# Sums of squares of the RMS norms: full-array matmuls against partial sums in the four column quarters of TensorE

## The reference, cut to what matters

```python
def _rmsnorm(x, w):
    xf = x.astype(jnp.float32)
    y = xf * lax.rsqrt(jnp.mean(xf * xf, axis=-1, keepdims=True) + RMS_EPS)
    return (y * w.astype(jnp.float32)).astype(x.dtype)

h = h + _mixer(_rmsnorm(h, norm_mix_w[l]), ...)          # norm 0
h = h + _swiglu(_rmsnorm(h, norm_ffn_w[l]), ...)         # norm 1
h = _rmsnorm(h, norm_final_w)                            # folded into norm 2
h = _rmsnorm_2(x, mix_norm_g[layer]); x = x + mixer(h)   # norms 2 and 4
h = _rmsnorm_2(x, mlp_norm_g[layer]); x = x + mlp(h)     # norms 3 and 5
```

## Time and profile before

| | |
|---|---|
| median of 3 runs | 1178.59 us (1178.41 to 1178.78) |
| profiled execution, its own time | 1178.25 us |
| its span in the profile | 1176.5 us |
| mean granted TensorE clock | 0.977 of full speed |
| PE busy | 1122.0 us (95%) |
| DVE busy | 745.9 us (63%) |
| ACT busy | 508.6 us (43%) |

### The profile page before, as it was taken

The page is one execution under the profiler, slowest core; times in us unless marked ns, Lnnn a source line. Parts: engine busy times, 40 slices in busy tenths (PEclk is TensorE's granted clock), DMA queues, the critical chain, the costliest instruction groups (busy, mean ns, idle before and its releaser), DMA issues.

```text
span 1176.5 us, 21013 instructions
## 1 busy us (share of the span) xinstructions
PE 1122.0 (95%) x8656; PEld 1068.6 (91%) x8656; DVE 745.9 (63%) x813; ACT 508.6 (43%) x506; POOL 6.0 (1%) x6
## 2 busy tenths in 40 slices
PE   8999998899999999998998999999988999999998
PEld 7998885788989999988887999999978999999998
DVE  5764747576756666668746565555479776655563
ACT  5523332433544444455484444333443455434331
POOL 0000001000000000000000000000000000000000
PEclk8999999899999999999999999999898999999999
DMA  9673243134427565664423464654253435564630
GB/s 299 188 211 108 90 143 108 44 130 154 129 72 210 166 203 170 191 201 150 150 95 108 143 215 158 199 177 145 85 165 112 139 108 176 183 211 157 203 107 36
DMA packets 162590, 177.63 MB, mean 151 GB/s; under 512 B 4800, under 2 KB 148288, under 8 KB 162536
## 3 DMA queue, kind: packets, MB, share of 16 engines
q1 hardware_dynamic: 160704, 174.56, 46.9%
q10 hardware_dynamic: 1832, 2.30, 1.0%
HBM read 175.27 MB, written 1.57 MB: 150 GB/s over the span
## 4 chain that ended last, share of the span: by engine, by line
PE 79%; DVE 12%; ACT 5%; issue 2%; DMA 2%; ACTq 0%; SPq 0%; DVEq 0%
PE proj L417 48%; PE aux L778 20%; DVE wlo L1409 4%; DVE f L1412 2%; DVE f L1409 2%; PE aux L474 2%; ACT whi L1035 1%; PE aux L705 1%; DMA gamma_rows<-f 1%; DVE f L1415 1%; PE aux L688 1%; PE aux L585 1%; PE aux L574 1%; DMA f<-in_x_dram 1%; PE aux L698 1%
## 5 line engine op out<-in xcount | busy, mean ns | idle before, releaser
L417 PE MATMUL proj<-u,whi 128*128 128x256 f32 (+1 forms) x2912 | 538.7, 286 | 11.2 <-DVE wlo L1409 4.1
L1409 DVE TENSOR_TENSOR wlo<-raw,whi 128x2048 fp32r<-128x2048 f32 (+2 forms) x176 | 374.2, 2126 | 159.7 <-ACT whi L1035 151.7
L417 PEld LDWEIGHTS proj<-u,whi 128*128 128x128 f32 x2912 | 455.9, 191 | 20.3 <-issue 8.0
L417 PE MATMUL proj<-u,wlo 128*128 128x256 f32 (+1 forms) x1456 | 413.7, 284 | 0.0
L1035 ACT ACTIVATE whi<-raw 128x2048 fp32r<-128x2048 f32 (+3 forms) x174 | 311.6, 1791 | 124.8 <-PE proj L417 56.0
L417 PEld LDWEIGHTS proj<-u,wlo 128*128 128x128 f32 x1456 | 279.0, 192 | 0.0
L778 PE MATMUL aux<-v,whi 128*128 128x256 f32 x1376 | 249.9, 283 | 2.7 <-DVE v L1409 2.5
L778 PEld LDWEIGHTS aux<-v,whi 128*128 128x128 f32 x1376 | 214.2, 192 | 3.4 <-issue 3.4
L778 PE MATMUL aux<-v,wlo 128*128 128x256 f32 x688 | 194.6, 283 | 0.0
L778 PEld LDWEIGHTS aux<-v,wlo 128*128 128x128 f32 x688 | 131.9, 192 | 0.0
L417 PE MATMUL proj<-v,whi 128*128 128x256 f32 (+2 forms) x592 | 109.1, 286 | 6.5 <-DVE f L1409 3.4
(11 more groups left out here) (263 smaller groups left out, 752.3 us busy)
## 6 DMA issues: line engine op xcount, KB each, us to landing
raw<-in_mlp_w_dram SPq DMA_DIRECT2D x64, 1024.0 KB, 5.3
raw<-in_w_in_dram SPq DMA_DIRECT2D x21, 1024.0 KB, 6.9
raw<-in_od_w_in_dram SPq DMA_DIRECT2D x12, 1024.0 KB, 5.4
raw<-in_w_ffn_gate_dram SPq DMA_DIRECT2D x22, 512.0 KB, 3.9
raw<-in_w_ffn_up_dram SPq DMA_DIRECT2D x22, 512.0 KB, 5.2
raw<-in_w_ffn_down_dram SPq DMA_DIRECT2D x21, 512.0 KB, 5.3
raw<-in_ev_w_in_dram SPq DMA_DIRECT2D x10, 1024.0 KB, 5.6
raw<-in_w_ret_out_dram SPq DMA_DIRECT2D x4, 1024.0 KB, 5.3
```

What stands on the lines that cost most here:

```text
L417: ins = mm(o, w_of(a, k), x_of(b, k), start=first and k == 0 and j == 0, stop=last and k == kt - 1 and j == 2, skip_group_check=skip)
L1409: return ve.tensor_tensor(o, a, b, op)
```

## The change

`square_pair` sums tile k only into the column quarter k mod 4 of the array, 32 columns of ones wide, and so into 32 of the 128 partitions of `aux[:, 0]`. Tiles 0 to 3 start the sums of the four quarters and tiles 4 to 7 add to them. Then every partition holds the sum over two tiles. ScalarE copies the 128 partial sums to `r_all[:, 0]` (`parts_kept`), and one more full matmul of ones (`whole_sum`) adds them up over the partitions into `aux[:, 0]`. As each partial sum stands in 32 partitions, the root's scale gets a factor 1/32. `whole_sum` is issued between the two output blocks (j = 0 and 1) of the first projection behind the norm, in norm 0 between those of rq1. The second sums of norm 2 are as before.

```diff
             def square_pair(c, norm_no, tokens=S, second=False):
 
                 pe.wait_ge(sems["sq_ready"], 4 * norm_no + c + 1)
                 for k in (2 * c, 2 * c + 1):
-                    ins = mm(aux[:, 0, 0:tokens], C("ones"), sq_of(tokens)[:, k, :], start=k == 0, stop=k == KT - 1,
+                    part = slice(32 * (k % 4), 32 * (k % 4) + 32)
+                    ins = mm(aux[part, 0, 0:tokens], C("ones")[:, 0:32], sq_of(tokens)[:, k, :], start=k < 4, stop=k >= 4,
                              skip_group_check=True)
...
                 if c == 3:
-                    ins.then_inc(sems["sumsq"], 1)
+                    ins.then_inc(sems["sum_parts"], 1)
+
+            def whole_sum(norm_no, tokens=S):
+
+                pe.wait_ge(sems["parts_kept"], norm_no + 1)
+                mm(aux[:, 0, 0:tokens], C("ones"), r_all[:, 0, 0:tokens], start=True, stop=True).then_inc(sems["sumsq"], 1)
...
-            project("rq1", t0=META, t=S)
+            project("rq1", t0=META, t=S, between=lambda: whole_sum(0, L))
...
-                def up(n, k, i=None, gate=None):
+                def up(n, k, i=None, gate=None, between=None):
...
+                        if between and j == 0:
+                            between()
                     finish(ins)
...
-                up(g, 0, gate=by_pair(norm_no))
+                up(g, 0, gate=by_pair(norm_no), between=lambda: whole_sum(norm_no))
...
-            project("sq0", t0=META, t=S, gate=by_pair(2, second=True))
+            project("sq0", t0=META, t=S, gate=by_pair(2, second=True), between=lambda: whole_sum(2))
...
-            project_tokens("gates", 8, gate=by_pair(4))
+            project_tokens("gates", 8, gate=by_pair(4), between=lambda: whole_sum(4))
...
             pump(index["rq0"] - AHEAD + 2)
+            eng.wait_ge(sems["sum_parts"], 1)
+            A.post(act(r_all[:, 0, :], aux[:, 0, 0:L], ACT.Copy), "parts_kept")
             eng.wait_ge(sems["sumsq"], 1)
-            root(aux[:, 0, 0:L], r_all[:, 0, :], 1.0 / D, eps, "root_ready")
+            root(aux[:, 0, 0:L], r_all[:, 0, :], 1.0 / 32 / D, eps, "root_ready")
...
                     pump(loop_last[source] - 1)
+                eng.wait_ge(sems["sum_parts"], norm_no + 1)
+                A.post(act(r_all[:, 0, 0:S], aux[:, 0, 0:S], ACT.Copy), "parts_kept")
                 eng.wait_ge(sems["sumsq"], norm_no + 1)
-                root(aux[:, 0, 0:S], r_all[:, 0, 0:S], 1.0 / D, eps, "root_ready")
+                root(aux[:, 0, 0:S], r_all[:, 0, 0:S], 1.0 / 32 / D, eps, "root_ready")
```

More of the change, by code:

```diff
@@ L458, in project, with project_tokens @@
                 finish(ins)
-            def project_tokens(name, width=256, gate=None):
+            def project_tokens(name, width=256, gate=None, between=None):
                 n = index[name]
```

## The result

| | before | changed |
|---|---|---|
| median | 1178.59 us (1173.0 to 1179.25, 8 runs) | 1184.07 us (1182.67 to 1186.01, 8 runs) |
| profiled execution, its span | 1178.25 us, 1176.5 us | 1183.95 us, 1182.2 us |
| mean granted TensorE clock | 0.977 | 0.972 |

The ratio is 1.0059, with a 95% interval of 1.0044 to 1.0073: the change costs 6.9 us, 5.2 to 8.6. (The ratio is not the quotient of the two medians, which is 1.0046.) I had forecast 1180.5, 1.9 us slower, and a range up to 1183.4, so the direction was right and the size too small.

A forecast was written before the change was run, and what follows sets the result against it. TensorE was taken to bound most of the span, 79% of the chain. Terms +0.8 - 0.3 + 0.7 - 0.25 + 0.9 = +1.9 on 1178.25, median 0.34 above, gave 1180.5 us; range 1178.2 to 1183.4, eight times in ten.

The forecast's parts named there:

- What bounds the kernel, norms 1, 3 and 5: Norms 1, 3, 5: the sum's posting time counts, not TensorE's time; sum 0.1 us earlier each, -0.3 in all.
- Quarters overlap: In the squares of the norms: up to four quarter passes run at once, 0.215 us a round.
- rival C: In the norms' quarter rounds: weight loads don't overlap between quarters, so +2.6 us, 1183.1; chance 0.06.
- Norm 0, +0.8: Norm 0: whole sum behind rq1's first block of 24 matmuls, so root's table load 0.8 us later; bounds 0.5, 0.9.
- rival A: Norm 0: clock falls behind 4.1 us of idling instead of 1.41, costing 1.5 us on the chain, 1182.0; chance 0.28.
- Norm 2, +0.7: Norm 2: copy waits behind ScalarE's split, so VectorE's reciprocal starts 0.7 us later; bounds 0.6 to 0.8.
- The 0.25 given back by the clock: Behind norm 2: TensorE's next chunk starts later, so less runs at half clock, -0.25 us if the clock recovers when before.
- Norm 4, +0.9: Norm 4: clock stays low through the gates, recovers within qk0's first block at 856.6; factor turned 0.9 us later.
- the bound of +2.2: Norm 4: upper bound of its term, +2.2 us, if the clock stays low through qk0's block.
- The median shown: Whole kernel: base of the forecast, an execution of 1178.25 us with the median 0.34 above it.

The follow-up runs named there:

- e4: The changed kernel with quarter sums in norms 1, 3 and 5 only, the other norms with full squares; 1176.96 us, ratio 0.9996 to the kernel before.
- e5: Quarter sums in norm 0 only, plus eight unused matmuls of ones between rq1 and rk0; 1178.76 us, ratio 1.0015 to the kernel before.
- e1: The changed kernel with quarter sums in norm 0 only, norms 1 to 5 with full squares; 1178.78 us, ratio 1.0011 to the kernel before.
- e2: The changed kernel with quarter sums in norm 2 only, the other norms with full squares; 1177.08 us, ratio 1.0002 to the kernel before.
- e9: The change without norm 4, which keeps full squares, plus eight unused matmuls between rq1 and rk0; 1180.25 us, ratio 1.0028 to the kernel before.
- e14: The change in norms 1, 2, 3 and 5 only, norms 0 and 4 as before; 1177.69 us, ratio 1.0007 to the kernel before.
- e3: The changed kernel with quarter sums in norm 4 only, the other norms with full squares; 1179.43 us, ratio 1.0029 to the kernel before.
- e8: The kernel before with only norm 4 changed: full squares kept, copy and whole sum added, scale 1/128; 1177.89 us, ratio 1.0006.
- e12: The kernel before plus norm 0 quarters, whole sum ahead of rq1's k = 3 rows, fillers ahead of rk0, behind norm 2 and ahead of stick-breaking transposes; 1174.38 us, ratio 0.9982.
- e7: The kernel before, without quarters, plus two unread ScalarE copies ahead of norm 0's root; 1179.21 us, ratio 1.0021.
- e10: The kernel before, without quarters, plus eight unused matmuls of ones between sq0 and sq1 behind norm 2; 1176.38 us, ratio 0.9991.

## Why the prediction failed

The forecast was +1.9 us, the measured change +6.9. What the prediction said of the engines' own work in norms 0, 1, 2, 3 and 5 came out within 0.15 us. What failed is what it let TensorE's clock do, in two terms: norm 4 at +0.9, with the clock back in the middle of qk0's first block, and the fall in norm 0, for which the sum had nothing. With the measured stages in place of all terms (2.24 in norm 0, 0.69 in norm 2, 2.08 in norm 4, nothing in the others) the sum is 5.0; with norm 4 taken against the mean of its stage, 6.2.

*What bounds the kernel, norms 1, 3 and 5.* Right. TensorE's passes are saved and go into idle time; the sum is posted 0.03 later instead of 0.1 earlier, and the times show nothing of it (e4, -0.5 us, -1.9 to +1.1). The copy took 0.38, and 0.40 for 272 columns, instead of 0.47.

*Quarters overlap.* Right, against rival C. The Trainium skill ("TensorE: Matmul & The Clock Gate", section "The mechanism") says that loads overlap running matmuls only where the row group differs (earlier, the same section also has a load into the background weight buffer run ahead); here eight loads of all 128 rows into four column quarters lie within 0.16 us beside running matmuls, so the measurement decides against the "only".

*Norm 0, +0.8.* This is the second step that failed. The delay was right (0.75 in the change, 0.74 in e5 with the clock held), but its consequence stands in the sum at nothing: rival A, the clock's fall by the longer idle time, came at its price (rk0 takes 1.5 us longer in both traces of the change, 2.0 in e1), and I had given it 0.28. I had forecast the idle time at 4.1 us, as long as the one behind norm 2 that a fall followed, and set against it only that it might be shared between two busy stretches, for which none of my rows spoke. The Trainium skill (same page, section "HAM oscillation — how this bites in real kernels") says that bursts of matmuls with waits between them start at the half clock each time; the trace agrees, with 4.24 us of idling and 3.3 us at 0.50 behind it. By that rule the forecast would have been 1182.0.

*Norm 2, +0.7.* Right to 0.01. The 0.25 given back by the clock was wrong: in both traces of the whole change the clock stayed at half for 6.8 us there, in e2, e9 and e14 for 3.4. Where it falls next shifts from kernel to kernel, and I count neither as a cost of norm 2 alone.

*Norm 4, +0.9.* This is the first and larger step that failed: "I take it that the clock then stays low through the gates" was right, "then qk0's first block of 24, of which about 11 at 0.21 (up to 856.6)" was not. I let the clock recover at the time at which it had recovered before. It stayed at half to 863.4, through all of the block, so the profiled stage grew by 2.08, near the bound of +2.2 that I had for this case. On top of it I took the one execution of the kernel before as what norm 4 costs, and it was one of the long ones for that stage (16.85, with 15.50 in the mean). Against the mean the term is +3.2, outside my bounds. e3 and e8 show the cause of the larger part: without the dense passes of the full squares, which keep the clock up or bring it back, it stays at half through the gates and the block behind them. The rest is the copy and the whole sum.

*The median shown.* The three runs of before lay at 1178.59; larger groups gave 1176.1 to 1177.4. So the base of the forecast was 1.2 to 2.5 us too high, which by luck brought the 1180.5 nearer to the 1184.07: in the medians the miss is 3.6 us, by the ratio 5.0.

## What to carry to other kernels

A saving in TensorE's passes is only worth something where TensorE's time is what ends a stage; where it waits, the saved passes become idle time, and idle time ahead of a chunk can cost more than the saving: behind the 4.24 us of norm 0 the half clock cost 1.5 us, behind the 2.25 us of norm 1 nothing. Before taking dense passes out of a stretch of sparse ones, look at the granted clock of that stretch: they may be what keeps it up. Where a serial sum through another engine is to be earned back, put it as early as the data allow (in e12, with the gap behind it filled, the stage was 1.0 us shorter than before), and judge a clock effect over several executions, since one trace shows only one place of its falls.

## What the runs showed of the hardware

- Matmuls of 128 rows and 32 columns in the four column quarters ran four at a time with plain fp32 data: 16 in 1.12 us, at 272 moving columns, where 16 on the whole array took 3.83.
- An idle stretch of 2.28 us was followed by 3.4 us at half clock (e7), one of 1.41 (before) and one of 2.25 (the change, ahead of norm 1's down matmul) were not.
- A TensorE that shows as fully busy, first with matmuls of 8 columns and quarter passes and for some 5.7 us at the end with matmuls of 256 columns, stayed at half clock for 17.1 us (the change, e3); with sixteen passes on the whole array among the first of them it was 6.8 (e8).
- A half-clock stretch removed by filler work was made up by a longer one 30 us on (e10).
